# Moving the group softmax sum, the POOL zeroing and half of the low gather in a routed expert layer

## The reference

```python
def hier_moe(h, w_group, b_group, w_router, b_router, w_e_gate, w_e_up, w_e_down):
    g_logits = (hf @ w_group) + b_group          # 4 groups
    g_probs = jax.nn.softmax(g_logits, axis=-1)
    g_top = jnp.argmax(g_logits, axis=-1)
    g_w = jnp.take_along_axis(g_probs, g_top[:, None], axis=1)
    ...                                          # the 8 experts of that group, the best two of them
    e_w, e_idx = lax.top_k(jax.nn.softmax(e_logits, axis=-1), TOP_K)
    gates = g_w * e_w / e_w.sum(...)
    out = sum over experts e of gates[:, e] * ((silu(hf @ w_e_gate[e]) * (hf @ w_e_up[e])) @ w_e_down[e])
```

## Time and profile before

| | us |
|---|---|
| median of 3 runs | 1908.83 (1908.61 to 1909.7) |
| the profiled execution | 1911.17 |
| its span | 1909.3 |
| routing, from the logits copy to the last selection row | about 355.4 to 375.6 of the span |
| gather on the PE | 375.67 to 385.8 |
| expert tile 0 on the PE | 387.85 to 400.4 |
| expert tiles 1 to 34 | 400.4 to about 1000 |

### The profile page before, as it was taken

One profiled execution on the slowest core, in us unless ns is written; L12 is line 12 of the kernel. 1 busy time (PEld: TensorE's weight loads), 2 busy tenths in 40 slices (PEclk: granted clock), 3 DMA queues, 4 the chain that ended last, 5 costly groups with the idle time before them and its releaser, 6 DMA issues. The chain is left out here.

```text
span 1909.3 us, 30124 instructions
## 1 busy us (share of the span) xinstructions
PE 1759.8 (92%) x11594; PEld 1592.5 (83%) x11594; DVE 1356.6 (71%) x1457; ACT 1047.0 (55%) x1072; POOL 76.9 (4%) x104
## 2 busy tenths in 40 slices
PE   7999989799999999999984788989999979899998
PEld 7998869678777887778763688889999979799998
DVE  6455787688988888888975855576555867566554
ACT  4333565478888888888762254345334474344332
POOL 0000000130000000000004300000000010000000
PEclk9999999799999999999996889999999989999999
DMA  9651116279999999999992424345554535335540
GB/s 309 189 179 56 56 45 224 74 276 395 396 391 401 396 393 392 390 405 389 395 352 98 133 89 151 114 136 196 176 178 152 164 124 179 112 129 186 188 154 23
DMA packets 200408, 419.30 MB, mean 220 GB/s; under 512 B 7200, under 2 KB 152352, under 8 KB 182400
## 3 DMA queue, kind: packets, MB, share of 16 engines
q1 hardware_dynamic: 198656, 411.54, 59.7%
q0 software_dynamic: 1664, 6.52, 0.9%
HBM read 398.64 MB, written 19.40 MB: 219 GB/s over the span
## 5 line engine op out<-in xcount | busy, mean ns | idle before, releaser
L1566 DVE TENSOR_TENSOR wlo<-raw,whi 128x2048 fp32r<-128x2048 f32 (+1 forms) x377 | 856.9, 2274 | 269.1 <-ACT whi L1120 265.2
L1120 ACT ACTIVATE whi<-raw 128x2048 fp32r<-128x2048 f32 (+1 forms) x377 | 712.9, 1892 | 387.7 <-PE ps L589 259.1
L587 PE MATMUL ps<-xh,whi 128*128 128x256 f32 x1096 | 323.4, 295 | 41.3 <-DVE xl L1579 32.9
L588 PE MATMUL ps<-xl,whi 128*128 128x256 f32 x1096 | 316.9, 289 | 0.0
L589 PE MATMUL ps<-xh,wlo 128*128 128x256 f32 x1096 | 316.8, 289 | 0.0
L587 PEld LDWEIGHTS ps<-xh,whi 128*128 128x128 f32 x1096 | 216.9, 198 | 48.7 <-issue 44.3
L587 PE MATMUL ps<-xb_h,whi 128*128 128x256 f32 x768 | 218.6, 285 | 5.4 <-DVE arena L1648 5.4
L588 PE MATMUL ps<-xb_l,whi 128*128 128x256 f32 x768 | 218.1, 284 | 0.0
L589 PE MATMUL ps<-xb_h,wlo 128*128 128x256 f32 x768 | 218.0, 284 | 0.0
L588 PEld LDWEIGHTS ps<-xl,whi 128*128 128x128 f32 x1096 | 217.1, 198 | 0.4
L589 PEld LDWEIGHTS ps<-xh,wlo 128*128 128x128 f32 x1096 | 216.6, 198 | 0.1
(11 more groups left out here) (326 smaller groups left out, 2734.5 us busy)
## 6 DMA issues: line engine op xcount, KB each, us to landing
raw<-w_e_gate_dram SPq DMA_DIRECT2D x70, 1024.0 KB, 8.0
raw<-w_e_up_dram SPq DMA_DIRECT2D x70, 1024.0 KB, 7.8
raw<-w_e_down_dram SPq DMA_DIRECT2D x70, 1024.0 KB, 7.9
raw<-ffn_w_gate_up_dram SPq DMA_DIRECT2D x44, 1024.0 KB, 5.1
raw<-w_in_dram SPq DMA_DIRECT2D x31, 1024.0 KB, 5.5
raw<-ffn_w_down_dram SPq DMA_DIRECT2D x22, 1024.0 KB, 4.9
compact_y<-arena SPq DMA_DIRECT2D x35, 512.0 KB, 7.3
raw<-xa_w_kv_dram SPq DMA_DIRECT2D x16, 1024.0 KB, 5.4
```

Source lines behind the costliest of these rows:

```text
L587: mm = nc.tensor.matmul(o, wh, h, start=first and a == 0, stop=False, skip_group_check=not group)
L588: nc.tensor.matmul(o, wh, l, start=False, stop=False, skip_group_check=not group)
L1120: nc.scalar.activation(whi[u % HL][:, 0:n], raw[u % RAW][:, 0:n], ACT.Copy).then_inc(hi_ready, 1)
L1566: v.tensor_tensor(wlo[u % HL][:, 0:n], raw[u % RAW][:, 0:n], whi[u % HL][:, 0:n].bitcast(F32), ALU.subtract).then_inc(lo_ready, 1)
```

## The change

The group sum and its reciprocal, and with them DVE's wait for ACT's exponential, go behind the ranks, among the gate instructions. POOL starts its zeroing when the second gather chunk is done, not when the ranks are. Low chunks 4 to 7 go to banks 1, 3, 4 and 5 and are gathered between the first and the second product of expert tile 0; the first product waits for four low copies, the gather's second half for all high copies, the third product for all low ones.

```diff
--- before.py
+++ after.py
@@ -348,6 +348,12 @@
 
             at = g * T if len(step["scores"]) == 3 else g * 512
             return ps[:, at // 512, at % 512:at % 512 + step["nk"]]
+
+        def gather_bank(c, low):
+
+            if low:
+                return c if c < 4 else (1, 3, 4, 5)[c - 4]
+            return 4 + c % 4
 
         compact = nc.dram_tensor("compact_y", (WIDE, D), F32, kind="Internal").ap()
 
@@ -799,9 +805,9 @@
             def experts(p0):
                 def gather(c, low):
 
-                    o = ps[:, c % 4 if low else 4 + c % 4, :]
-                    if c >= 4:
-                        pe.wait_ge(gath_l if low else gath_h, c - 3)
+                    o = ps[:, gather_bank(c, low), :]
+                    if c >= 4 and not low:
+                        pe.wait_ge(gath_h, c - 3)
                     src = tok_l if low else tok_h
                     for tt in range(2):
                         mm = nc.tensor.matmul(o, src[:, tt, c * P:c * P + P], chosen_rows[:, tt, :], start=tt == 0,
@@ -871,13 +877,14 @@
                     gather(c, True)
                 for c in range(4, 8):
                     gather(c, False)
+                pe.wait_ge(gath_l, 4)
+                h, l = xc_h[:, :, 0:P], xc_l[:, :, 0:P]
+                product(0, p0, h[:, 0:4, :], l[:, 0:4, :], True, False)
+                pe.wait_ge(gath_h, 8)
                 for c in range(4, 8):
                     gather(c, True)
-                pe.wait_ge(gath_h, 8)
+                product(2, p0 + 1, h[:, 0:4, :], l[:, 0:4, :], True, False)
                 pe.wait_ge(gath_l, 8)
-                h, l = xc_h[:, :, 0:P], xc_l[:, :, 0:P]
-                product(0, p0, h[:, 0:4, :], l[:, 0:4, :], True, False)
-                product(2, p0 + 1, h[:, 0:4, :], l[:, 0:4, :], True, False)
                 product(0, p0 + 2, h[:, 4:8, :], l[:, 4:8, :], False, True)
                 product(2, p0 + 3, h[:, 4:8, :], l[:, 4:8, :], False, True)
 
@@ -1250,7 +1257,7 @@
             def experts(p0):
                 def gathered(c):
                     act.wait_ge(gath_mm, c + 1 if c < 4 else c + 5)
-                    nc.scalar.activation(xc_h[:, c, 0:PAIRS_OUT], ps[:, 4 + c % 4, :], ACT.Copy).then_inc(gath_h, 1)
+                    nc.scalar.activation(xc_h[:, c, 0:PAIRS_OUT], ps[:, gather_bank(c, False), :], ACT.Copy).then_inc(gath_h, 1)
 
                 def row_start(m, i=None):
                     at = start_i[0:1, m:m + 1] if i is None else start_i[0:1, bass.ds(i * LOOP + m, 1)]
@@ -1787,7 +1794,7 @@
             def experts(p0):
                 def gathered(c):
                     dve.wait_ge(gath_mm, c + 5 if c < 4 else c + 9)
-                    v.tensor_copy(xc_l[:, c, 0:PAIRS_OUT], ps[:, c % 4, :]).then_inc(gath_l, 1)
+                    v.tensor_copy(xc_l[:, c, 0:PAIRS_OUT], ps[:, gather_bank(c, True), :]).then_inc(gath_l, 1)
 
                 def row_start(m, i=None):
                     at = start_i[0:1, m:m + 1] if i is None else start_i[0:1, bass.ds(i * LOOP + m, 1)]
@@ -2052,10 +2059,6 @@
 
             first_max(col(12, 4), gl, N_GRP, gkeys, 0, 8, 3)
             v.tensor_tensor(col(4, 4), gl, wide(0, 4), ALU.subtract).then_inc(route_grp, 1)
-            dve.wait_ge(route_grp_exp, 1)
-            link(v.tensor_reduce(col(1), col(4, 4), AX.X, ALU.add))
-            link(v.reciprocal(col(2), col(1)))
-
             link(v.tensor_scalar(col(16, 4), col(12, 4), -FAR, FAR, ALU.mult, ALU.add))
             for a in range(2):
                 pen = rt[:, a, 16:20].unsqueeze(2).broadcast_to([P, N_GRP, 8])
@@ -2107,7 +2110,9 @@
             link(v.tensor_copy(start_i[:, 0:N_EXP], starts[:, 0, :]))
             dve.sem_inc(starts_there, 1)
             dve.wait_ge(route_two_exp, 1)
+            v.tensor_reduce(col(1), col(4, 4), AX.X, ALU.add)
             link(v.tensor_scalar(col(25), col(24), 1.0, None, ALU.add))
+            v.reciprocal(col(2), col(1))
             link(v.reciprocal(col(25), col(25)))
             link(v.tensor_tensor(gates[:, :, 0:1], col(25), col(2), ALU.mult))
             link(v.tensor_tensor(gates[:, :, 1:2], gates[:, :, 0:1], col(24), ALU.mult))
@@ -2289,7 +2294,7 @@
 
             g = nc.gpsimd
 
-            pool.wait_ge(ranks_mm, 1)
+            pool.wait_ge(gath_mm, 2)
             link(g.memset(zeros, 0.0))
             wide_zeros = zeros.unsqueeze(1).broadcast_to([P, DC, P])
             g.tensor_copy(xc_h[:, :, PAIRS_OUT:], wide_zeros).then_inc(tails_set, 1)
```

## The result

The changed kernel takes 1897.89 us (median of 6 runs, 1896.93 to 1900.19) against 1909.26 us (6 runs) of the kernel before on the same chip: ratio 0.9945, 95% interval 0.9935 to 0.9955, so 8.6 to 12.4 us faster. Over all runs of this study it is a mean of 1898.6 (12 runs) against 1909.4 (55 runs), 10.8 us faster (9.7 to 11.8, resampled). Forecast were 8.2 us and 1900.6, with a range from 1899.0.

A forecast was written before the change was run, and what follows sets the result against it. The PE, busy 92% of the span, was taken to set the pace, so only its stops or half clock could be won. Parts A, B and C, 3.9 + 1.5 + 2.8 = 8.2 us, gave a median of 1900.6, range 1899.0 to 1904.0.

The forecast's parts named there:

- the head start at tile 1: Expert loop: the PE sets the pace, so time won by tile 1 should live until the end.
- Rivals 2 and 4: Experts: 2, DMA sets the pace, gain 3.4 to 5.4 us (0.07); 4, another loop rhythm, 5.4 us slower (0.04).
- rival 5: Whole change: edits do nothing, another wait takes over in each place, 1908 us; chance 0.06.
- Part A: Routing: group sum and reciprocal moved behind the ranks; ranks and row numbers 3.9 us sooner, bounds 3.9 and 4.7.
- rival 3: Routing: rank products free of the transposes or clock rises sooner, gain 9 to 10 us, 1899.3 us; chance 0.09.
- Part B: Routing: POOL's zeroing moved later, DVE's subtraction and scan no longer stretched; 1.5 us, range 1.1 to 1.6.
- Cost 0 to 0.3 us, I take 0: POOL's new place: casts may hold small DVE instructions, ending the four low copies up to 1 us later.
- Part C: Gather and tile 0: second low gather half between products, less standing still and half clock; 2.8 us, bounds 1.1 and 3.85.
- Rival 1: Before tile 1: the clock falls once more at the new 0.8 us stop, price 1.7 us, 1902.3 us; chance 0.14.
- A term was left at nothing: Gather: clock rising 1.4 us sooner or later would move the low chunks some 0.7 us; counted as nothing.

The follow-up runs named there:

- after_again: The changed kernel run once more with no edit: 1899.36 us (5 runs), ratio 0.9942.
- after_look: The changed kernel, one more profiled look with no edit: one run of 1897.92 us.
- after: First measurement and profile of the changed kernel against the kernel before: median 1897.89 us, ratio 0.9945; profiled execution 1896.93 us.
- after_fill: The changed kernel plus nine unread matmuls on the PE ahead of the token transposes: 1899.30 us, ratio 0.9944.
- gates_late: The reorder kernel with tile 1's row number loaded before the second four low copies and gate instructions behind the residue of p0+4: 1898.27 us, ratio 0.9942.
- a_only: The kernel before with only the group sum and reciprocal moved behind the ranks: 1902.36 us, ratio 0.9964.
- reorder: The changed kernel with weight unit p0+2 opened and its residue made ahead of the copies of chunks 4 to 7: 1898.42 us, ratio 0.9948.
- b_only: The kernel before with only POOL's zeroing made to wait for the second gather chunk: 1906.74 us, ratio 0.9984.
- c_only: The kernel before with only the second half of the low gather put between the first two products, in other banks: 1905.40 us, ratio 0.9983.
- before: The kernel before the change, first measurement and profile: 1909.26 us (6 runs).
- before_again: The kernel before, run once more with no edit: 1907.14 us.
- before_look: The kernel before, one more look with no edit: 1908.55 us.
- before_fill: The kernel before plus nine unread matmuls on the PE between the logits' and the tokens' transposes: 1908.34 us, ratio 0.9994.
- gates_late_fill: The gates_late kernel plus unread matmuls, nine between logits' and tokens' transposes and twelve between ranks and gather: 1896.49 us, ratio 0.9927.

## Why the forecast was too small

- **What bounds it, and the head start at tile 1.** Right. What was won by tile 1 was there at the end of the loop (585.0 us from tile 1's transpose to the last one before, 584.6 to 586.0 in all others), and ACT waited for no load in it. Rivals 2 and 4 are out (and rival 5, as the median moved by 11.4 us): the pace held, and the loop's end, counted from the logits copy, was 9.6 us sooner in the first pair, not 3.4 to 5.4.
- **Part A, the step that failed.** "The ranks move from 366.52 to 362.6: 3.9 us ... and the row numbers at 368.90 follow them." The term took the transposes' 3.68 us and the ranks' 2.38 us as lengths of the work, but they are its lengths at half clock in one execution. At half clock it measured 4.1 us for the ranks and 4.2 for the row numbers (after_again, after_look); at full clock 4.8 and 5.8 (after, after_fill). I had 4.7 as the upper bound, and no term at all for the ranks' own length. Term by term, where 3.9 + 1.5 + 2.8 = 8.2 was forecast, after_look gives 4.2 + 1.5 + 3.0, some 8.8, and after 5.8 + 1.5 + 2.6 = 9.9. My rival 3 named the course, at 9 to 10 us in all, and gave it 0.09; of the six profiles with part A and nothing added to the PE ahead of the transposes, two took the whole of that course (after, gates_late), one a part (a_only), and three did not (after_again, after_look, reorder).
- **Part B.** Right: 1.5 us forecast, 1.5 measured (after, b_only); subtraction 0.19, scan 0.29 (0.27 estimated). The scan's excess was 0.76 us, 0.78 was taken. At the new place L2109 took 0.97 us and L2114 0.69 beside POOL's casts. The rule of the Trainium skill cited in the forecast ("SBUF — State Buffer", the section on the two sides of the memory) agrees for such conversions and scalar operations. For the PSUM copies no run shows it: where POOL zeroes late, the low copies begin only after its casts have ended (372.56 against 371.83 in after). The holding cost the first low copies the 1.09 us in which DVE had waited and 0.4 us more. In the change the first product waits for that by 0.1 us at most; in b_only, where the low chunks came sooner, the PE stood 3.20 us (above). The forecast's "Cost 0 to 0.3 us, I take 0" held with part C's order; b_only has the old one.
- **Part C.** Right in each wait and in size: 2.8 us forecast, 2.6 (after), 3.1 (after_again), 2.9 (c_only). Rival 1, another fall of the clock, took place in none of the profiles. The 1.66 us of half clock that it removes were lost in all five profiles with the old order of gather and tile 0 and the old place of the sum, but not in a_only, after a longer stop: this share doesn't simply add to part A.
- **The rest.** From the routing to tile 1 the profiles give 8.8 to 10.0 us, the times 10.8 (9.7 to 11.8). The profiles of the change without edits average 9.2, some 1.6 us less than the times. So of the 2.6 us by which the times exceed the forecast, the profiles show 0.6 (routing at half clock) to 1.7 (at full clock). I can't say where the rest is: the time up to the logits copy varies by 2.9 us among all these profiles, and "end" by 3.0, with no tie to the change. The clock has a part in it: the seven of the change's twelve runs with a mean clock of 0.968 or 0.969 took 1896.9 to 1899.4 us, the five with 0.965 or 0.966 took 1898.6 to 1903.0, and the kernel before shows 0.961 to 0.966. That doesn't say in which stage, so it stays open.
- **The range.** It was built from bounds of the edits alone. A term was left at nothing, "the clock rises within the gather at a point that needn't keep its distance", with 0.7 us either way; the eight low matmuls took 2.37 to 3.00 us in the change and 2.83 to 2.94 before, so it was worth up to 0.5 us. The change's own six runs spread over 3.3 us, and the clock's part in the routing alone is 1.2 us to one side. The lower end should have reached 1897.

## What to carry to other kernels

A duration read from the trace at half clock is no length of the work. Before a sum rests on it, look at PEclk over that row, work the sum out at either clock, and ask what hid the faster course before: a wait that ended last in the old order can hide a slack that the new order cashes. A stop removed from one engine was replaced here by that engine's next instruction in line (a residue, then a register load). A few matmuls whose result nobody reads kept the clock up where they lay in the gap ahead of the gather and delayed nothing: 1.8 us in the profile, 1.5 to 4.1 in the times. Those ahead of the transposes brought nothing that the times show.

## What the runs showed of the hardware

- The same program with the same work takes the transposes in 1.97 or 3.68 us, after the same stop of 2.73 or 2.74 us. Nor does the length of a stop alone decide ahead of tile 0: 2.02 to 2.15 us (before, before_again, before_look, before_fill) and 3.20 us (b_only) lost the clock, 2.31 us kept it (a_only). A stop of 2.49 us behind twelve matmuls kept it ahead of the gather (gates_late_fill).
- A DVE conversion of 4 elements per partition took 0.97 us beside a POOL cast, six times its 0.16 us, and ended with the cast; a sum over 8 elements per partition beside such a cast took its usual 0.16 us. An operation that reads PSUM and one SBUF array was not stretched: in gates_late_fill the four of `xl` take 0.74 us each, the last one beside POOL's cast, as in before without one.
- DVE stood 1.03 us where a row number is loaded into a register directly ahead of its use (reorder); with the load ahead of other work the stop was gone (gates_late).
